# Turning activations for a transformer trunk's MLPs: 32x32 blocks on VectorE and a pass through DRAM, in place of TensorE transposes

## The reference

```python
def rmsnorm(x, g):
    y = x32 * lax.rsqrt(jnp.mean(jnp.square(x32), axis=-1, keepdims=True) + RMS_EPS)
    return (y * g.astype(jnp.float32)).astype(x.dtype)
def sqrelu_mlp(h, w_up, w_down):
    return jnp.square(jax.nn.relu(h @ w_up)) @ w_down
for layer in range(DEPTH):
    h = h + (fox_mixer, retention_mixer)[layer](rmsnorm(h, ...), ...)
    h = h + sqrelu_mlp(rmsnorm(h, mlp_norm[layer]), mlp_up[layer], mlp_down[layer])
return rmsnorm(h, final_norm)
```

## Time and profile before

| what | value |
|---|---|
| median of three runs | 2549.94 us |
| the profiled execution | 2546.82 us, span 2544.6 us, mean granted clock 0.999 |
| TensorE busy | 2525.5 us, 99% |
| VectorE busy | 1874.3 us, 74% |
| ScalarE busy | 1425.0 us, 56% |
| DMA queue of SyncE | 476.65 MB, 53.2% of 16 engines |
| longest wait of TensorE in total, by line | 3.9 us |

### The profile page before, as it was taken

The page is one execution under the profiler, slowest core; times in us unless marked ns, Lnnn a source line. Parts: engine busy times, 40 slices in busy tenths (PEclk is TensorE's granted clock), DMA queues, the critical chain, the costliest instruction groups (busy, mean ns, idle before and its releaser), DMA issues.

```text
span 2544.6 us, 30524 instructions
## 1 busy us (share of the span) xinstructions
PE 2525.5 (99%) x11490; PEld 2085.0 (82%) x11490; DVE 1874.3 (74%) x2110; ACT 1425.0 (56%) x1745; POOL 32.1 (1%) x42
## 2 busy tenths in 40 slices
PE   9999999999999999999999999999999999999998
PEld 7888887888888888888888888887888888888887
DVE  6455555787877787887777877777887777778786
ACT  7444444555646556655556546555565565564564
POOL 0000000000000000000000000000000000000000
PEclk9999999999999999999999999999999999999999
DMA  8445456464555555455654655556555554546463
GB/s 306 153 154 175 138 194 214 150 232 165 213 184 204 193 207 190 169 185 182 205 197 165 224 191 180 182 180 212 185 214 200 199 198 180 217 159 237 149 238 126
DMA packets 133333, 486.58 MB, mean 191 GB/s; under 512 B 15056, under 2 KB 15312, under 8 KB 132304
## 3 DMA queue, kind: packets, MB, share of 16 engines
q1 hardware_dynamic: 131328, 476.65, 53.2%
q0 software_dynamic: 1728, 7.87, 0.9%
q10 hardware_dynamic: 144, 0.26, 0.0%
HBM read 482.63 MB, written 2.10 MB: 190 GB/s over the span
## 4 chain that ended last, share of the span: by engine, by line
PE 99%; DVE 0%; ACT 0%; issue 0%; DMA 0%; SPq 0%; DVEq 0%; ACTq 0%
PE acc L798 13%; PE acc L800 13%; PE acc L799 13%; PE sc L800 12%; PE sc L798 12%; PE sc L799 12%; PE acc L579 4%; PE acc L581 4%; PE acc L580 4%; PE tr L597 2%; PE mix L798 2%; PE mix L800 2%; PE mix L799 2%; PE sc L694 0%; PE tr L944 0%; PE mix L636 0%
## 5 line engine op out<-in xcount | busy, mean ns | idle before, releaser
L1806 DVE TENSOR_TENSOR w_lo<-raw,w_hi 128x1024 fp32r<-128x1024 f32 x694 | 849.0, 1232 | 364.1 <-ACT w_hi L1237 361.5
L1237 ACT ACTIVATE w_hi<-raw 128x1024 fp32r<-128x1024 f32 x694 | 732.6, 1059 | 636.4 <-PE sc L800 223.6
L798 PE MATMUL acc<-w_hi,xT_hi 128*128 128x512 f32 x826 | 323.8, 392 | 2.1 <-DVE h L1748 1.7
L800 PE MATMUL acc<-w_hi,xT_lo 128*128 128x512 f32 x826 | 321.9, 390 | 0.0
L799 PE MATMUL acc<-w_lo,xT_hi 128*128 128x512 f32 x826 | 321.6, 389 | 0.0
L1806 DVE TENSOR_TENSOR w_lo<-scratch,w_hi 128x1024 fp32r<-128x1024 f32 x203 | 247.0, 1222 | 95.5 <-ACT w_hi L1237 94.7
L1237 ACT ACTIVATE w_hi<-scratch 128x1024 fp32r<-128x1024 f32 x203 | 214.1, 1059 | 179.0 <-PE sc L800 69.7
L798 PE MATMUL sc<-w_hi,xT_hi 128*128 128x512 f32 x736 | 290.7, 395 | 0.0
L800 PE MATMUL sc<-w_hi,xT_lo 128*128 128x512 f32 x736 | 287.2, 390 | 0.0
L799 PE MATMUL sc<-w_lo,xT_hi 128*128 128x512 f32 x736 | 286.6, 389 | 0.0
L798 PE MATMUL acc<-w_hi,aT_hi 128*128 128x512 f32 x600 | 234.8, 391 | 3.5 <-issue 3.5
(11 more groups left out here) (252 smaller groups left out, 3871.8 us busy)
## 6 DMA issues: line engine op xcount, KB each, us to landing
raw<-in_w_stream SPq DMA_DIRECT2D x725, 512.0 KB, 4.5
scratch<-in_w_stream SPq DMA_DIRECT2D x170, 512.0 KB, 5.2
gain<-in_gains POOLq DMA_DIRECT2D x4, 1024.0 KB, 7.5
h<-in_x SPq DMA_DIRECT2D x2, 1024.0 KB, 8.9
scratch<-in_gn POOLq DMA_DIRECT2D x8, 256.0 KB, 4.4
scratch<-in_x_t SPq DMA_DIRECT2D x3, 512.0 KB, 8.8
scratch<-in_decay POOLq DMA_DIRECT2D x8, 192.0 KB, 3.1
out<-raw SPq DMA_DIRECT2D x1, 1024.0 KB, 3.9
```

The source lines that it names most:

```text
L798: pe.matmul(bank[:, :], x_hi, w_hi[:, c], start=start, stop=False, skip_group_check=True)
L800: return pe.matmul(bank[:, :], x_lo, w_hi[:, c], start=False, stop=stop, skip_group_check=True)
L1237: act.activation(w_hi[:, slot * SW:(slot + 1) * SW], mlp_raw(u, load_of(u, t)), ACT.Copy).then_inc(mlp_hi, 1)
L1806: dve.tensor_tensor(w_lo[:, c], mlp_raw(u, load_of(u, t)), w_hi[:, c].bitcast(F32), ALU.subtract).then_inc(mlp_lo, 1)
```

## The change

From the end of layer 0's first mixer on, the quads of hidden values of both MLPs, three of the four quads of the retention's norm and all four of the second MLP's norm are turned another way; 39 quads of both token tiles ("turns"). All other transposes stay.

The values to be turned are now written to the PSUM banks `tr` (one tensor of both banks, 128 x 1024). VectorE transposes their 32x32 blocks into `stage` (`turn_blocks`, one instruction of 1024 columns). SyncE stores `stage` to DRAM (`park_turn`, 512 KB), waits for it, and reads it back with the blocks in their places, by four DMAs of 128 KB, in pieces of 256 neighbouring elements (`fetch_turn`), into `evac`. ScalarE makes the high part (`turn_hi`) and VectorE the low part (`turn_lo`), both of 1024 columns in one instruction. TensorE has no batch there, and waits for `turn_out`. `place_turns` says between which weight loads SyncE puts a park and a fetch: those of the first turn of a pair in front of the load that waits for tile 6, the park of the second one in front of the load that waits for tile 8, its fetch in front of the one that waits for tile 11. The squares of h for the norm get a buffer of their own (`junk`).

```diff
+TB = 32
+GRID = P // TB
+UP_TURNS, RET_TURNS = SUPER * QUADS, QUADS - 1
+RET_NORM_AT = UP_TURNS
+MLP_NORM_AT = RET_NORM_AT + RET_TURNS
+UPS_AT = (0, MLP_NORM_AT + QUADS)
+TURNS = UPS_AT[1] + UP_TURNS
...
+def turn_of_pair(m, i):
+    if i == 0:
+        return MLP_NORM_AT + 2 if m else None
+    if i == PAIRS - 1:
+        return None if m else RET_NORM_AT
+    return UPS_AT[m] + (i - 1) // 4 * QUADS + (i - 1) % 4 * 2 if (i - 1) % 4 < 2 else None
...
+def staged_before(n):
+    return QUADS + n + 1 + (2 * RET_HEADS + 1 if n >= MLP_NORM_AT else 0)
...
+def place_turns():
+    parked, fetched = [0] * TURNS, [0] * TURNS
+    def put(n, u, t, u2, t2):
+        parked[n], fetched[n] = UNITS[u].tiles + t + 1, UNITS[u2].tiles + t2 + 1
+    for m in range(2):
+        for i in range(PAIRS):
+            n, u = turn_of_pair(m, i), mlp_unit(m, i)
+            if n is None:
+                continue
+            if (m, i) == (0, 1):
+                put(n, u - 1, 2 * SLOTS - 1, u, TAU1)
+            else:
+                put(n, u, TAU3, u, TAU2)
+            put(n + 1, u, SEVEN + 1, u, SEVEN + 4)
+    put(RET_NORM_AT + 2, head_unit(0), 2, head_unit(0), 4)
+    put(MLP_NORM_AT, wo_unit(1, 1), TAU3, wo_unit(1, 1), TAU2)
+    put(MLP_NORM_AT + 1, wo_unit(1, 1), SEVEN + 1, wo_unit(1, 1), SEVEN + 4)
+    return parked, fetched
...
+        stage_both, evac_both = sb("stage", TOKS * NB), sb("evac", TOKS * NB)
+        stage, evac = ([part[:, t * NB:(t + 1) * NB] for t in range(TOKS)] for part in (stage_both, evac_both))
...
+        def in_toks_and_tiles(part, quad):
+            quads = part[:, :].rearrange("p (t d) -> p t d", t=TOKS)[:, :, quad * NB:(quad + 1) * NB]
+            return quads.rearrange("p t (j a r) -> p t j a r", j=NB // P, a=GRID)
+        fetched_tiles = evac_both[:, :].rearrange("p (a t j r) -> p t j a r", a=GRID, t=TOKS, j=NB // P)
...
+        tr_both = ctx.enter_context(nc.psum_tensor("tr", [P, TOKS * NB], F32))
+        tr = [tr_both[:, t * NB:(t + 1) * NB] for t in range(TOKS)]
...
+        park = nc.dram_tensor("park", (TURNS, P, TOKS * NB), F32, kind="Internal").ap()
...
+            def park_turn(n):
+                sp.wait_ge(turned, n + 1)
+                sp.dma_start(park[n], stage_both[:, :]).then_inc(parked, 16)
+            def fetch_turn(n):
+                sp.wait_ge(parked, 16 * (n + 1))
+                wait(sp, turn_out, n)
+                rows = park[n].rearrange("(a c) (b k) -> b c a k", a=GRID, b=GRID)
+                for g in range(GRID):
+                    sp.dma_start(evac_both[g * TB:(g + 1) * TB, :].rearrange("p (a k) -> p a k", a=GRID),
+                                 rows[g]).then_inc(fetched, 16)
...
+                        while free_at and fetches < TURNS and (PARKED_AT, FETCHED_AT)[parks > fetches][fetches] <= free_at:
+                            if parks == fetches:
+                                park_turn(parks)
+                                parks += 1
+                            else:
+                                fetch_turn(fetches)
+                                fetches += 1
+                        if free_at:
+                            sp.wait_ge(mlp_lo, free_at)
...
+            def seven_pair(u, lhs, between, turned=False, after_block=False, heads_done=0, end=False, first_turn=None):
                 unit, up = UNITS[u], lhs is xT
                 x, z, e, w = banks_of(u)
+                if first_turn is not None:
+                    pe.wait_ge(turn_out, first_turn + 1)
...
+                    if first_turn is not None and s % 2 == 0:
+                        pe.wait_ge(turn_out, first_turn + 2 + s // 2)
...
             def mlp_pair(m, i):
-                last = m == 1
-                up, was_up = i % 4 < 2, i > 0 and (i - 1) % 4 < 2
-                normed = i >= PAIRS - 2 and not last
-                was_normed = i == PAIRS - 1 and not last or m == 1 and i == 0
-
-                def between(t):
-                    if was_up and t == B21 or was_normed and t == TAU2:
-                        own()
-                    if was_up and t == B22 or was_normed and t == TAU4:
-                        pending()
-                    if t == SEVEN + REST + (1 if up else 2) and (up or normed):
-                        own()
-                    if t == SEVEN + REST + (2 if up else 3) and (up or normed):
-                        pending()
-
-                seven_pair(mlp_unit(m, i), xT if up else aT, between, turned=not up or i == 0,
-                           heads_done=RET_HEADS * m, end=last and i == PAIRS - 1)
+                first_turn = (UPS_AT[m] + i // 4 * QUADS if i % 4 == 2 else MLP_NORM_AT if m == 1 and i == 0 else None)
+                seven_pair(mlp_unit(m, i), xT if i % 4 < 2 else aT, lambda t: None, heads_done=RET_HEADS * m,
+                           end=m == 1 and i == PAIRS - 1, first_turn=first_turn)
...
+                    elif hd == 0 and s % 2 == 0:
+                        pe.wait_ge(turn_out, RET_NORM_AT + 1 + s // 2)
...
-                act.activation(evac[tok][:, :], evac[tok][:, :], ACT.Relu).then_inc(relu_made, 1)
+                act.activation(tr[tok], tr[tok], ACT.Relu).then_inc(relu_made, 1)
                 act.wait_ge(relu_made, T("relu"))
-                act.activation(stage[tok][:, :], evac[tok][:, :], ACT.Square).then_inc(staged[tok], 1)
+                act.activation(tr[tok], tr[tok], ACT.Square).then_inc(staged[tok], 1)
...
+            def turn_hi(n, dst, quad):
+                act.wait_ge(fetched, GRID * 16 * (n + 1))
+                act.activation(in_toks_and_tiles(dst, quad), fetched_tiles, ACT.Copy).then_inc(turn_hi_made, 1)
...
+                if turn is not None:
+                    turn_hi(turn, dst, p_quad)
                 if was_normed:
                     square_of_h(1, p_quad + 1, w_out, done)
+                hi(u, 8)
+                hi(u, 9)
                 if new_sums:
                     s_high(new_sums, was_normed)
-                hi(u, 8)
-                hi(u, 9)
-                if was_up or was_plain:
-                    batch_hi(0, aT_hi, p_quad + 1)
-                hi(u, 10)
-                if was_normed and not end:
-                    batch_hi(0, xT_hi, p_quad + 1)
-                hi(u, 11)
-                if was_up or was_plain:
-                    batch_hi(1, aT_hi, p_quad + 1)
-                hi(u, 12)
-                if was_normed and not end:
-                    batch_hi(1, xT_hi, p_quad + 1)
-                hi(u, 13)
+                for t in range(10, 14):
+                    hi(u, t)
                 if was_head:
                     batch_hi(0, aT_hi, QUADS - 1)
                 hi(u, 14)
                 if was_head:
                     batch_hi(1, aT_hi, QUADS - 1)
+                if turn is not None:
+                    turn_hi(turn + 1, dst, p_quad + 1)
...
+            def turn_blocks(n):
+                for t in range(TOKS):
+                    dve.wait_ge(staged[t], staged_before(n))
+                wait(dve, parked, 16 * n)
+                dve.transpose(stage_both[:, :].rearrange("p (b m r) -> p m b r", b=GRID, r=TB),
+                              tr_both[:, :].rearrange("p (m b c) -> p m b c", b=GRID, c=TB)).then_inc(turned, 1)
+            def turn_lo(n, dst_hi, dst_lo, quad):
+                dve.wait_ge(turn_hi_made, n + 1)
+                dve.tensor_tensor(in_toks_and_tiles(dst_lo, quad), fetched_tiles,
+                                  in_toks_and_tiles(dst_hi, quad).bitcast(F32), ALU.subtract).then_inc(turn_out, 1)
+            def turned_sums(n):
+                s = [mlp_sums[:, k * 2 * P:(k + 1) * 2 * P].rearrange("p (j a r) -> p j a r", j=2, a=GRID)
+                     for k in range(4)]
+                (a11, a12), (a21, a22) = ([fetched_tiles[:, t, j:j + 2] for j in (0, 2)] for t in range(TOKS))
+                dve.wait_ge(fetched, GRID * 16 * (n + 1))
+                step(dve.tensor_tensor(s[S1], a21, a22, ALU.subtract))
+                step(dve.tensor_tensor(s[S2], a11, s[S1], ALU.subtract))
+                dve.tensor_tensor(s[S3], a11, a21, ALU.subtract)
+                dve.tensor_tensor(s[S4], a12, s[S2], ALU.subtract).then_inc(s_made, 1)
...
                 tau2(u)
-                if was_plain:
-                    s_sums(aT_hi, aT_lo)
+                if turn is not None and not was_plain:
+                    turn_blocks(turn)
                 lo(u, TAU3)
...
+                    dve.wait_ge(turned, turn + 1)
+                    sum_to(tr[0], sc[0], v_sum, e_done, e_out, done)
...
                 lo(u, 7)
                 if was_head:
                     gated_out(hd, 0)
-                if new_sums:
-                    s_low(new_sums, was_normed)
+                if turn is not None:
+                    turn_blocks(turn + 1)
                 lo(u, 8)
                 if was_head:
                     gated_out(hd, 1)
+                if new_sums:
+                    turned_sums(turn)
```

(32 more changed lines are left out.)

137 lines of the change are left out of this document (49 added, 88 removed).

## The result

The changed kernel takes 2623.2 us (median of four, 2619.2 to 2628.9) against 2549.2 before: ratio 1.029 [1.027, 1.032]. The forecast was 2547, the range ended at 2562. The profiled execution took 2626.1 us (span 2624.2).

A forecast was written before the change was run, and what follows sets the result against it. TensorE, busy 99% of 2544.6 us, was taken as the bound. 2546.8 - 36.7 (batches removed) + 36.2 (nine waits) = 2546.3, so 2547 us, no change; the range ran from 2534, less 1, to 2562.

The forecast's parts named there:

- The 36.7 us removed: On TensorE, 78 transpose batches at 0.47 us each go, 36.7 us, all of it on the path.
- Where TensorE waits: TensorE waits for turned quads at tile 11 of eight first down pairs and in the second MLP's first pair: 36.2 us.
- hd 0's block: First query-key block of the retention: quad 2, due at 10.9 us, was found ready at about 7.
- VectorE alone ready at 22.9: First down pair: VectorE's order alone ends quad 3's low part at 22.9 us, 2.5 late, whatever the transfers do.
- C: Rival: longer block transpose or low part makes VectorE bound the second up pairs; 2554 to 2557 us; chance 0.18.
- With the park's 512 KB ahead of it, load 13 lands at 20.1, the fetch's 512 KB behind it at about 21.6: SyncE's queue, first down pair: backlog moves 1.27 us per 512 KB; TensorE then restarts at 24.2, 3.8 after 20.4.
- 36.2: TensorE's nine waits together: 8 x 3.8 = 30.4 us in first down pairs, 5.8 in the second MLP's first pair.
- The fetch's price: Fetch in 1 KB pieces: at least 1.27 us, at most 5.1; taken near the lower end, 1.5.
- Restart at full clock: TensorE after a wait: starts 0.1 us after VectorE's end, with a product of 0.47 instead of 0.39.
- B: Rival: transfers are hidden and VectorE alone sets the stall, 2.7 us nine times, 24; 2534 us; chance 0.27.
- D: Rival: the fetch pays by the piece, 5.1 us each, stalls +32; 2579 us, half way 2562; chance 0.10.
- The two signs: Forecast wrong if pairs without a wait don't shrink to 42.2 us, or if TensorE never waits at tile 11.

The follow-up runs named there:

- run 10: Changed kernel, but TensorE keeps the fourth quads of the up products and of MLP 1's first pair, batches behind tiles TAU4 and 7: 2522.0 us, ratio 0.990.
- Run 1: Changed kernel without the DRAM trip: VectorE transposes into two SBUF buffers in turn, copies read them there, blocks not in their places: 2542.1 us, ratio 0.997.
- Run 14: Changed kernel, but the fetch's four transfers each take a quarter of the columns of all 128 rows, in 1 KB pieces: 2580.0 us, ratio 1.013.
- 15: Changed kernel, but the fetch's four transfers each take 32 whole rows, every fourth row instead of neighbouring ones: 2587.0 us, ratio 1.016.
- Run 5: Changed kernel, but the fetch's four transfers of 32 neighbouring rows bring whole rows, 4 KB pieces instead of 1 KB: 2618.8 us, ratio 1.028.
- run 13: Changed kernel, but TensorE runs 36 products into an unread bank ahead of the wait for the fourth quarter in nine pairs: 2602.1 us, ratio 1.021.

## Why the prediction was wrong, step by step

- **The 36.7 us removed: right.** Pairs without a wait went to 42.16 as forecast; the kept batches of run 10 cost 0.47 again.
- **Where TensorE waits: right.** Tile 11 of eight first down pairs and of the first pair of MLP 1. Missed was hd 0's block, called ready at about 7: 5.9 us.
- **VectorE alone ready at 22.9: right.** Run 1 restarts at 22.8. The block transpose took 1.24 us, and what follows it starts 1.17 behind it, for 1.15 assumed: C doesn't occur. (The Trainium skill's one element per cycle, in Vector Engine (DVE) Microarchitecture Reference, "The reshape front-end and per-opcode configuration", gives an estimate of 1.07; the trace is 0.10 above it from start to start.) In the first pair of MLP 1, which the forecast took to be like the others, run 1 restarts at 24.65.
- **"With the park's 512 KB ahead of it, load 13 lands at 20.1, the fetch's 512 KB behind it at about 21.6": mis-sized.** Run 14 shows this step without the narrow rows. In pair 2 of MLP 1 tile 7 is on time and the park is issued at 9.5 as forecast, but it lands at 17.3 for 16.4, load 13 at 22.05, the fetch at 23.4. The fetch costs 1.36 behind the load, as I had it. In the eight first down pairs load 13 lands at 21.7 in the mean, where 18.9 and the 1.27 of the park had given 20.2. Of this 0.9 stands ahead of the park already: the load in front of it lands at 16.0 in the mean, 15.1 before the change; what slows the queue there stays open. The park itself costs what I had allowed, two times 1.27 between the loads on either side of it, unless something else falls there: in the nine pairs each of runs 14, 15 and the changed kernel these loads land 2.5 to 2.6 us apart in fifteen and 2.8 to 4.1 in twelve, and in each of the twelve a packet of 16 KB of the instruction queue falls between, 0.95 us long or a little more (of the fifteen only one has such a packet, at its very end). Here they are 3.4 apart, and the queues from 16.5 to 19.0 after the start of the pair (packets, MB, share of 16 engines) show it:

```profile
q1 hardware_dynamic: 272, 0.99, 99.7%
q8 instruction: 1, 0.02, 2.4%
```

That the packet is the cause is argued from these 27 pairs, not tested. TensorE restarts at 25.8 for 24.2, and the nine waits sum to 50.6 for 36.2: **14 us**.

- **The fetch's price: wrong in kind.** I had bounded it by the size of its pieces and taken 1.5 us. Run 5 says that pieces cost some 4 us at most, runs 14 and 15 that 32 neighbouring rows cost: changed less run 14 is 31.5 + 9.3 + 5.9, less 0.8 of tile 11: **46 us** (43 by the medians). Part of it is indirect: the second up pairs' fetches, slow in the same way, keep VectorE and ScalarE standing, w_lo of tile 7 starts at 9.2 instead of the 7.10 "as before", and the park follows at 11.6 instead of 9.5.
- **Restart at full clock: wrong, and never weighed.** I had read the restart from the earlier trace rows, after 1.7 us of idleness, where the product took 0.47. Behind the waits here tile 11 takes up to twice its time: 18.3 us here, 2.4 in run 13, and 8.3 even in run 1, which is why B's 2534 was really 2542.

Together 36.2 + 14.4 + 46 + 19 (run 14's tile 11) + 1 = 116.6, the 116.6 of the account. B fell since nothing hides the transfers; D, at 2579, came nearest, but by a mechanism that doesn't exist here. My range allowed for each cost alone, but they all fall on the same nine waits and add up. The two signs that were to show the forecast wrong (pairs that don't shrink to 42.2, no wait at tile 11) didn't come; what did were waits of 7.6 to 11.9 us in place of 3 to 4.5.

## What to carry to other kernels

Before work is moved to a round trip, find the one place where its result is needed soonest, and leave the old way there: here 18 of 78 batches kept, with the copies of the other turns moved behind tile 18 where they had time, make +3% into -1%. Read a hop in a backlog from what stands ahead of it in bytes, whoever issues it, and leave some room, since the same queue was 0.9 us later here than in the trace of before. And count a wait of TensorE with its tail: behind one, tile 11 took up to 5.3 us for 2.72.

## What was not expected of the hardware

- Transfers into 32 neighbouring rows cut a full queue from 368 to 229 GB/s in the pair shown, and the loads among them slow too. 1 KB against 4 KB pieces made little or no difference (2623.2 and 2618.8 us).
- Whether tile 11 comes slow isn't decided by the wait's length alone: after a wait of 2.4 us in all eight pairs of run 1 it took 2.9 us in five of them and 4.3 to 4.5 in three.
- An issue by SyncE takes 0.44 us from DRAM and 0.63 from SBUF to SBUF.
- A 16 KB packet of the instruction queue among the loads goes with a delay of 0.3 to 1.5 us of the transfers around it (the twelve pairs above).
- Open: why the loads ahead of the park land 0.9 us later than before the change, and how a transfer of 32 neighbouring rows slows those of other rows.
